# A two-layer encoder trunk on one core: the depthwise taps divided anew, the first blocks in halves, the last columns apart

## The chip, the cores and the metric

The kernel runs on one core of a Trainium2 chip. Its time is the device time of one execution in microseconds (us); lower is better. In the profile PE is TensorE's matmuls (PEld its weight loads), DVE is VectorE, ACT is ScalarE, POOL is GpSimd and SP is SyncE, which here only issues DMAs.

## The reference, cut to what matters

All data are float32: 256 tokens of width 1024, two layers. Layer 0 mixes tokens by a convolution module, layer 1 by latent attention; each layer then has a PEER expert mixer, and each of the four sub-layers ends in a layer norm.

```python
def conv_module(x, w_in, b_in, w_dw, b_dw, ln_g, ln_b, w_out, b_out):
    h = x @ w_in + b_in                                    # (256, 2048)
    a, gate = jnp.split(h, 2, axis=-1)
    h = a * jax.nn.sigmoid(gate)
    h = lax.conv_general_dilated(                          # causal, depthwise, 31 taps
        h, w_dw[:, None, :], window_strides=(1,), padding=[(CONV_WIDTH - 1, 0)],
        dimension_numbers=('NWC', 'WIO', 'NWC'), feature_group_count=D_MODEL) + b_dw
    h = jax.nn.silu(layer_norm(h, ln_g, ln_b))
    return h @ w_out + b_out

for i in range(DEPTH):                                     # DEPTH = 2
    mix = conv_module(x, ...) if i % 2 == 0 else mla_mixer(x, ...)
    x = layer_norm(DEEPNORM_ALPHA * x + mix, ln1_g[i], ln1_b[i])
    ff = peer(x, peer_w_q[i], peer_sub_keys[i], peer_u[i], peer_v[i])
    x = layer_norm(DEEPNORM_ALPHA * x + ff, ln2_g[i], ln2_b[i])
```

`peer` scores 8 heads against 128 x 128 product keys, takes the best 16 experts of each head, and combines their rows of `u` and `v`; the kernel does this densely over all 16384 experts, and that is where most of its time goes.

## The kernel before, in words

**One program for each engine.** The order of each engine's work is written out by hand, in one function per engine; semaphores join them. Every engine takes its instructions strictly in that order, so an instruction that waits holds everything behind it in its program.

**The stream of weight blocks.** All weights come in 128 x 1024 blocks of 512 KB, numbered through the whole program: `conv_in` is 0 to 15, `conv_out` 16 to 23, `wq0` 24 to 39, then `u0`, `v0`, and layer 1's. SP loads block c into the landing buffer `raw[c % 3]`. ACT rounds it to a "high" half (`make_high(c)`, line 978), DVE or POOL subtracts that to a "low" half (`make_low(c)`, line 483; 503, 1667, 1671 and 1674 for the halves of the first two blocks), and PE uses both: each product is high x high, high x low and low x high. SP issues the load of block c only when block c - 3 has been read by both:

```python
sp.wait_ge(high_made, c - RING + 1)          # RING = 3
sp.wait_ge(low_made[c % RING], c // RING)
load(name, c)
```

So a low half made later is a load issued later. The finished halves lie in a ring of three or, for some blocks, in spare room ("far homes", the tile `far_homes`).

**The start.** The input x comes in four parts (`xT_in`), block 0 in two halves, block 1 in two halves. PE warms up on `ones` (line 716), projects block 0, with four more such matmuls in the middle of it, then blocks 1 to 15 (line 594). An even block holds a chunk of values, the odd one behind it the chunk's gates: eight chunks of 128 channels. ACT takes the sigmoid (line 1067), DVE multiplies (`glu`, line 1681).

**The taps.** Each chunk then needs 31 taps, one multiply-add over 256 tokens for each tap. Chunks 0 to 4 are on DVE (lines 1689 and 1691), in two lanes that alternate; the lanes share chunk 4, and line 1731 adds its two sums. Chunks 5 and 6 are on PE, as products with diagonal matrices (line 739) that ACT's queue loads (`big<-diag`, line 1055). Chunk 7 is on POOL: ACT makes each tap's product (line 1091) into one of six buffers, and POOL adds them in two alternating sums (line 512; 515 joins them). The DMAs that ACT issues behind the projection (diagonals, x, the norm's rows: lines 1055, 1073, 996) stand ahead of those products in its program.

**Between taps and norm.** PE transposes the eight chunks to rows (line 725), DVE measures them in four groups of two chunks (line 1736), normalises (line 1754); PE transposes back (line 732), ACT applies silu (line 1104) and rounds (line 1110), DVE makes the low halves (line 1763). ACT makes the highs of blocks 20 to 24 between its silu groups, POOL the lows of 17 to 21 and 23.

**conv_out and the first layer norm.** `combine_tail` (line 662) makes the tokens in two halves: half 0 of all eight blocks, then the left 512 columns of half 1, then its right 512. DVE's `layer_norm` runs add, measure, variance, centre (line 1366), reciprocal, scale (line 1370), and PE transposes x to columns (`turn_part`, line 699). ACT rounds these (line 1010), DVE makes their lows (line 1409). PE goes on with the first four blocks of `wq0` (`lead`, line 640), half 0 and then half 1. ACT's part of this stage, with `ready` = block 30 for the first norm, is

```python
std(n, 0)
if n == 0:
    highs_to(FIRST["wq0"] + LEAD["wq0"] - 1)      # to block 27
split_xT(n, 0)
if n % 2 == 0:
    highs_to(ready - 1)                           # 28, 29
    std(n, 1)
    highs_to(ready)                               # 30
...
split_xT(n, 1)
```

`std(n, 1)` gives the square root that half 1's scaling waits for, and `split_xT(n, 1)` rounds half 1's columns.

**The end.** The last norm runs the same way. DVE adds and measures half 1's right 512 columns when PE is done, then centres and scales both sides; each side is stored by a DMA of its own (lines 471 and 475).

## Time and profile before

| | us |
|---|---|
| median of three runs | 1806.12 (1806.07 to 1806.15) |
| the profiled execution's own time | 1807.27 |
| its span in the trace | 1805.5 |
| PE busy in the span | 1791.5 (99%) |
| PE weight loads | 1570.1 (87%) |
| DVE, ACT, POOL busy | 1366.3, 945.6, 212.6 |
| mean granted TensorE clock | 0.999 of full |

The span is the traced part of the profiled execution; 1.8 us of that execution lie around it. Times of single instructions below are from the span's start. PE's busy time also counts the matmuls on `ones` that fill waits, so a stage in which PE reads busy may still be one in which another engine sets the pace.

### The profile page before, as it was taken

The numbers are of one execution on the slowest core, as the hardware profiler recorded it, in microseconds if no ns is written. First come the engines' busy times: TensorE is split into PE (matmuls) and PEld (weight loads), VectorE is DVE, ScalarE is ACT, GpSimd is POOL, SyncE is SP. The second block draws the span as 40 slices with busy tenths as digits, with TensorE's granted clock in tenths as the row PEclk, the third lists the DMA queues.
The fourth block names the chain that finished last, engine by engine and source line by source line (L and its number), as shares of the span: only waits on it lengthen the run. The fifth ranks groups of instructions, "written<-read, shape, count | busy, mean of one in ns | idle before, by whom it ended". The sixth has DMA issues, their size and how long they took to land.

```text
span 1805.5 us, 28004 instructions
## 1 busy us (share of the span) xinstructions
PE 1791.5 (99%) x10622; PEld 1570.1 (87%) x10622; DVE 1366.3 (76%) x2461; ACT 945.6 (52%) x1489; POOL 212.6 (12%) x122
## 2 busy tenths in 40 slices
PE   9999999999999999999999999999999999999998
PEld 9889998888888888888888899988888888888886
DVE  7975999888986665666666669998889866666665
ACT  5565445555555455555535454555555554555552
POOL 6720930000000000000004048000000000000000
PEclk9999999999999999999999999999999999999999
DMA  7544555555556566667733346555555566666772
GB/s 240 184 152 153 186 174 168 165 172 166 169 171 211 192 195 195 199 219 245 241 111 116 111 152 195 170 161 171 165 175 164 175 212 196 193 192 207 220 217 79
DMA packets 89413, 323.89 MB, mean 179 GB/s; under 512 B 10048, under 2 KB 10560, under 8 KB 89024
## 3 DMA queue, kind: packets, MB, share of 16 engines
q1 hardware_dynamic: 85248, 307.42, 53.3%
q10 hardware_dynamic: 4032, 14.68, 2.3%
q8 instruction: 85, 1.39, 0.3%
q14 instruction: 48, 0.39, 0.1%
HBM read 321.01 MB, written 1.05 MB: 178 GB/s over the span
## 4 chain that ended last, share of the span: by engine, by line
PE 89%; DVE 7%; DMA 1%; issue 1%; ACT 1%; POOL 0%; SPq 0%; DVEq 0%; ACTq 0%
PE y L662 40%; PE work L553 19%; PE work L556 10%; PE work L594 9%; PE y L934 3%; DVE y L1691 3%; PE work L612 2%; PE y L640 2%; PE work L615 1%; PE work L802 1%; PE y L907 1%; DMA raw<-conv_in 1%; DMA raw<-v 0%; DVE far_homes L483 0%; DMA raw<-u 0%
## 5 line engine op out<-in xcount | busy, mean ns | idle before, releaser
L483 DVE TENSOR_TENSOR low<-raw,high 128x1024 fp32r<-128x1024 f32 x385 | 470.6, 1224 | 136.8 <-ACT high L978 132.2
L978 ACT ACTIVATE high<-raw 128x1024 fp32r<-128x1024 f32 x431 | 453.5, 1053 | 198.3 <-PE work L556 97.6
L553 PE MATMUL work<-xT,high 128*128 128x512 f32 x1472 | 374.0, 396 | 0.1
L662 PE MATMUL y<-high,xT 128*128 128x512 f32 x1296 | 352.6, 390 | 0.0
L553 PEld LDWEIGHTS work<-xT,high 128*128 128x128 f32 x1472 | 264.1, 189 | 47.6 <-DVE low L483 0.5
L662 PE MATMUL y<-far_homes,xT 128*128 128x512 f32 x1320 | 304.8, 390 | 0.2 <-DVE xT L1603 0.2
L662 PEld LDWEIGHTS y<-far_homes,xT 128*128 128x128 f32 x1320 | 247.1, 188 | 51.7 <-DVE far_homes L483 0.6
L662 PEld LDWEIGHTS y<-high,xT 128*128 128x128 f32 x1296 | 243.0, 188 | 50.2
L1244 ACT ACTIVATE xT<-big 128x256 fp32r<-128x256 f32 x256 | 105.3, 416 | 256.8 <-PE y L662 251.4
L556 PEld LDWEIGHTS work<-xT,low 128*128 128x128 f32 x1472 | 200.8, 190 | 14.6
L556 PE MATMUL work<-xT,low 128*128 128x256 f32 x1472 | 205.0, 282 | 0.0
L662 PE MATMUL y<-low,xT 128*128 128x512 f32 x648 | 200.9, 389 | 0.0
L978 ACT ACTIVATE far_homes<-raw 128x1024 fp32r<-128x1024 f32 x149 | 156.8, 1052 | 78.9 <-DMA raw<-v 32.9
L483 DVE TENSOR_TENSOR far_homes<-raw,far_homes 128x1024 fp32r<-128x1024 f32 x118 | 144.2, 1224 | 61.8 <-ACT far_homes L978 61.6
L1603 DVE TENSOR_TENSOR xT<-big,xT 128x256 fp32r<-128x256 f32 x256 | 107.5, 424 | 97.0 <-ACT xT L1244 96.9
L594 PE MATMUL work<-xT,high 128*128 128x256 f32 x960 | 174.7, 284 | 1.7 <-POOL low L483 0.8
L594 PEld LDWEIGHTS work<-xT,high 128*128 128x128 f32 x960 | 149.8, 192 | 2.9 <-POOL low L483 1.0
L662 PEld LDWEIGHTS y<-low,xT 128*128 128x128 f32 x648 | 121.6, 188 | 25.4
L594 PE MATMUL work<-xT,low 128*128 128x256 f32 x480 | 135.9, 283 | 0.0
L1234 ACT ACTIVATE cross<-work 128x512 f32<-128x512 f32 x92 | 55.0, 598 | 151.3 <-PE work L556 151.3
L483 POOL TENSOR_TENSOR low<-raw,high 128x1024 fp32r<-128x1024 f32 x46 | 112.1, 2447 | 159.8 <-ACT high L978 159.6
L594 PEld LDWEIGHTS work<-xT,low 128*128 128x128 f32 x480 | 92.2, 192 | 0.0
(208 smaller groups left out, 1818.8 us busy)
## 6 DMA issues: line engine op xcount, KB each, us to landing
raw<-u SPq DMA_DIRECT2D x256, 512.0 KB, 3.6
raw<-v SPq DMA_DIRECT2D x256, 512.0 KB, 4.3
raw<-wq SPq DMA_DIRECT2D x32, 512.0 KB, 3.7
raw<-conv_in SPq DMA_DIRECT2D x14, 512.0 KB, 4.4
aux<-ln_par ACTq DMA_DIRECT2D x9, 512.0 KB, 6.5
raw<-conv_out SPq DMA_DIRECT2D x8, 512.0 KB, 4.0
raw<-mla_out SPq DMA_DIRECT2D x8, 512.0 KB, 4.7
big<-diag ACTq DMA_DIRECT2D x6, 512.0 KB, 6.2
```

The costliest lines, as they stand in the source:

```text
L483: ops.tensor_tensor(low_at(c), raw[:, slot, :], high_at(c).bitcast(F32), ALU.subtract).then_inc(low_made[slot], 1)
L553: nc.tensor.matmul(both, w_high[:, cols], xT[:, k], start=(k == 0), stop=False)
L556: mm = nc.tensor.matmul(both[:, 0, :], w_low[:, cols], xT_high[:, k, :], start=False, stop=(k == KD - 1))
L594: mm = nc.tensor.matmul(out_, w[:, cols], m[:, k, :], start=(k == 0 and n == 0), stop=(k == KD - 1 and n == 2))
L612: nc.tensor.matmul(both, w_high[:, cols], xT[:, k], start=(k == 0), stop=False)
L662: mm = nc.tensor.matmul(y[:, 2 * h + m, :], a[:, a_slot, rows], v[:, m * 512:(m + 1) * 512], start=(start and n == 0), stop=(stop and n == 2))
L934: mm = nc.tensor.matmul(y[:, 2 * q + t // 4, cols], onehots[:, q, 2, token], onehots[:, q, part, token], start=(part == 0), stop=(part == 1))
L978: A(high_at(c), raw[:, slot, :], ACT.Copy).then_inc(high_made, 1)
L1234: A(cross[:], work[:, pair_banks(pair), T:2 * T], ACT.Copy).then_inc(cross_ok, 1)
L1244: A(xT_high[:, (c - v0) % KD, :], big[:, c - v0, :], ACT.Copy).then_inc(a_high, 1)
L1603: V.tensor_tensor(xT_low[:, n % KD, :], big[:, n, :], xT_high[:, n % KD, :].bitcast(F32), ALU.subtract).then_inc(a_low, 1)
L1691: return V.scalar_tensor_tensor(dst, padded[:, k, w:w + T], tap(k, w), total, ALU.mult, ALU.add)
```

## The change

It has four parts.

**The first blocks.** Blocks 0, 1 and 2 all come in halves, in the order x part 0, block 0 left, x part 1, block 1 left, x part 2, block 0 right, x part 3, block 1 right, then block 2's halves. PE runs left halves of blocks 0 and 1, then their right halves; the four matmuls in between are gone. ACT loads its sigmoid table ahead of the first sigmoid. The low of block 3 moves from POOL to DVE, behind DVE's first tap.

**The taps.** POOL gets chunk 6 and eleven other taps: nine of chunk 4 and the last two of chunk 7. PE gets the first 29 taps of chunk 7. DVE keeps 22 of chunk 4's 31. ACT makes the first nine products (chunk 4's) between the last blocks of the projection. A new instruction on DVE, `add_last`, joins chunk 7's two parts and its bias. The highs of blocks 17, 18 and 19 move between products.

**The first layer norm.** Half 1's left columns are added and measured ahead of `split_xT(0, 0)`; the low of block 26 (`wq0` + 2) moves from before that split to behind it, the low of block 27 from before half 1's norm to behind its first scaling.

**The end.** The last norm's half 1 is cut at column 768 instead of 512; its right 256 columns are summed in a bank of `work`.

```diff
-PE_CHUNKS = (5, 6)
-POOL_CHUNK = 7
+PE_CHUNKS = (5, 7)
+POOL_CHUNK = 6
-SHARED, SHARED_TAPS = 4, 22
+SHARED, SHARED_TAPS, SHARED_END = 4, 17, 22
+LAST_END = 29
+POOL_TAPS = ([(SHARED, _w) for _w in range(SHARED_END, TAPS)] + [(POOL_CHUNK, _w) for _w in range(TAPS)]
+             + [(PE_CHUNKS[1], _w) for _w in range(LAST_END, TAPS)])
+PRODUCTS_AT = {13: 6, 14: 8, 15: 9}
+HIGHS_AT = (12, 18, 24)
+LAST_FROM = 768
...                                        (SP)
+            def load_side(c, part, ready):
+                sp.dma_start(raw[:, c, sides[part]], blocks["conv_in"][c][:, sides[part]]).then_inc(ready, 16)
             for part in range(X_PARTS):
                 ks = slice(X_PART * part, X_PART * (part + 1))
                 sp.dma_start(xT_in[:, ks, :], x_cols[:, ks, :]).then_inc(xT_in_ok[part], 16)
+                c, side = part % 2, part // 2
+                load_side(c, side, landed[c] if side else (first_landed, second_landed)[c])
...                                        (POOL)
-            low_stage(3, FIRST["conv_out"] + 1)
+            low_stage(4, FIRST["conv_out"] + 1)
+            tap_sums(0, FOR_SHARED, 2, 0)
+            nc.gpsimd.tensor_tensor(pool_sums[:, 2, :], pool_sums[:, 2, :], pool_sums[:, 3, :],
+                                    ALU.add).then_inc(pool_step, 1)
+            tap_sums(FOR_SHARED, TAPS, 0, FOR_SHARED - 1)
+            nc.gpsimd.tensor_tensor(pool_sums[:, 3, :], products[:, last % PRODUCTS, :],
+                                    products[:, (last + 1) % PRODUCTS, :], ALU.add).then_inc(pool_last, 1)
...                                        (PE, the last half)
+                for n in range(TAIL):
+                    columns(n, 0, 512, y[:, 2, :], False, n == TAIL - 1)
+                    mm = columns(n, 512, LAST_FROM, y[:, 3, 0:LAST_FROM - 512], False, n == TAIL - 1)
+                mm.then_inc(y_left, 1)
+                for n in range(TAIL):
+                    columns(n, LAST_FROM, D, work[:, 0, 0:D - LAST_FROM], n == 0,
+                            n == TAIL - 1).then_inc(block_used, 1)
...                                        (PE, the taps)
-                for w in range(TAPS):
+                end = (TAPS, LAST_END)[c]
+                for w in range(end):
...
-            pe.wait_ge(pe_conv_ok, 2)
+            pe.wait_ge(conv_done, SHARED + 2)
             to_rows(PE_CHUNKS[1]).then_inc(rows_mm, 1)
...                                        (ACT)
-                make_high(t + RING)
+                if 0 < t < 2 * KD - 2:
+                    highs_to(t + RING)
+                if t in PRODUCTS_AT:
+                    products_to(PRODUCTS_AT[t])
...                                        (DVE)
+            def add_last():
+                k = PE_CHUNKS[1]
+                dve.wait_ge(pe_conv, 2)
+                dve.wait_ge(pool_last, 1)
+                V.scalar_tensor_tensor(conv[:, k, :], y[:, 1, 0:T], conv_p[:, C_BDW + k:C_BDW + k + 1],
+                                       pool_sums[:, 3, :], ALU.add, ALU.add).then_inc(conv_done, 1)
             for g in range(GROUPS):
+                if g == 2:
+                    add_last()
...
                     scale(sides[0])
+                    if n == 0:
+                        low_stage(FIRST["wq0"] + 3, FIRST["wq0"] + LEAD["wq0"])
                     centre(sides[1])
...
                 layer_norm(n, 0, end, bias_in=(layer == 0))
+                layer_norm(n, 1, end, bias_in=(layer == 0), left=True)
+                split_xT(n, 0)
                 if layer == 0:
                     low_stage(FIRST["wq0"] + 2, FIRST["wq0"] + 3)
-                if layer == 1:
-                    layer_norm(n, 1, end, left=True)
-                split_xT(n, 0)
-                if layer == 0:
-                    low_stage(FIRST["wq0"] + 3, FIRST["wq0"] + LEAD["wq0"])
-                    layer_norm(n, 1, end, bias_in=True, left=True)
                 layer_norm(n, 1, end, bias_in=(layer == 0))
```

DVE's program around the first layer norm, from the scaling of half 0 to the splits of half 1. Before (line 483 is a low half: here of blocks 26 and 27; 1358 adds, 1363 measures, 1366 centres, 1370 scales, 1409 splits):

```order
L1370 SCALAR_TENSOR_TENSOR x<-x,stats,aux 128x1024 [waits vector_step]
L483 TENSOR_TENSOR far_homes<-raw,far_homes 128x1024 [waits high_made]
L1409 TENSOR_TENSOR xT<-work,xT 128x4x128 [waits xT_high_made] x2
L483 TENSOR_TENSOR far_homes<-raw,far_homes 128x1024 [waits high_made]
L1358 TENSOR_TENSOR x<-x,y 128x512 [waits second_half_left_columns_combined]
L1363 BN_STATS stats<-x 128x6 [waits vector_step]
L1358 TENSOR_TENSOR x<-x,y 128x512 [waits block_used]
L1363 BN_STATS stats<-x 128x6 [waits vector_step]
L1388 BN_AGGR stats<-stats 128x2 [waits vector_step]
```

Now (489 is a low half, 1420 adds, 1426 measures, 1429 centres, 1433 scales, 1464 is the reciprocal, 1479 splits):

```order
L1420 TENSOR_TENSOR x<-x,y 128x512 [waits second_half_left_columns_combined]
L1426 BN_STATS stats<-x 128x6 [waits vector_step]
L1479 TENSOR_TENSOR xT<-work,xT 128x4x128 [waits xT_high_made] x2
L489 TENSOR_TENSOR far_homes<-raw,far_homes 128x1024 [waits high_made]
L1420 TENSOR_TENSOR x<-x,y 128x512 [waits block_used]
L1426 BN_STATS stats<-x 128x6 [waits vector_step]
L1455 BN_AGGR stats<-stats 128x2 [waits vector_step]
L1457 TENSOR_SCALAR stats<-stats 128x1 [waits vector_step]
L1429 SCALAR_TENSOR_TENSOR x<-x,stats,aux 128x512
L1464 RECIPROCAL stats<-stats 128x1 [waits std_made,vector_step]
L1433 SCALAR_TENSOR_TENSOR x<-x,stats,aux 128x512 [waits vector_step]
L489 TENSOR_TENSOR far_homes<-raw,far_homes 128x1024 [waits high_made]
```

The low of block 26 has gone from ahead of the splits to behind them, and the low of block 27 from ahead of half 1's sums to behind the scaling that waits for ACT's square root. ACT's rows for this stage read the same before and now.

ACT's program from the last gate of the projection to the products behind it. Before (1067 is the sigmoid, 978 a high, 1055, 1073 and 996 DMAs, 1091 a tap's product):

```order
L1067 ACTIVATE big<-work,big 128x256 [waits block_used]
L978 ACTIVATE high<-raw 128x1024 [waits block_used,block_landed_0]
L1055 DMA big<-diag 128x896
L1055 DMA big<-diag 128x1024 x3
L1073 DMA x<-x_rows 128x1024 x2
L996 DMA aux<-ln_par 128x1024 x3
L1091 ACTIVATE big<-big 128x256 [waits glu_made]
L1091 ACTIVATE big<-big 128x256 x5
L1091 ACTIVATE big<-big 128x256 [waits pool_step] x2
L978 ACTIVATE far_homes<-raw 128x1024 [waits block_landed_1]
```

Now, from the first product on (1127 is the sigmoid, 1020 a high, 1095, 1136 and 1038 DMAs, 1116 a product):

```order
L1116 ACTIVATE big<-big 128x256 x5
L1116 ACTIVATE big<-big 128x256 [waits pool_step,block_used]
L1116 ACTIVATE big<-big 128x256 [waits pool_step]
L1127 ACTIVATE big<-work,big 128x256 [waits block_used]
L1116 ACTIVATE big<-big 128x256 [waits pool_step]
L1095 DMA big<-diag 128x896
L1095 DMA big<-diag 128x1024 x3
L1136 DMA x<-x_rows 128x1024 x2
L1038 DMA aux<-ln_par 128x1024 x3
L1116 ACTIVATE big<-big 128x256 [waits pool_step,glu_made]
L1116 ACTIVATE big<-big 128x256 [waits pool_step] x2
L1020 ACTIVATE high<-raw 128x1024 [waits block_used,block_landed_2]
```

Chunk 4's nine products stand ahead of the nine DMAs, chunk 6's products behind them, as chunk 7's did; the first moved high stands behind chunk 6's third product.

## Rows read from the trace of the kernel before

**Rows 1.** Waits of PE over the span: waiter, releaser: us, times, longest.

```profile
PE work L725 <- DVE big L1731: 1.6, 1, 1.6
PE work L699 <- DVE x L1370: 0.6, 1, 0.6
```

**Rows 2.** Chain that ended last, 0 to 110 us: start, duration, work.

```profile
17.63 0.50 DVE big L1681
...
85.57 0.42 DVE big L1731
```

**Rows 3.** Timeline of all engines, 14 to 19 us: start, busy, operation, count [idle before].

```profile
14.68 1.06 ACT L978 ACTIVATE high<-raw 128x1024 fp32r<-128x1024 f32 x1 [1.69 <-DMA raw<-conv_in]
...
18.25 0.51 PE L594 MATMUL work<-xT,high 128*128 128x256 f32 x2 [0.81 <-POOL low L483]
```

**Rows 4.** Timeline of DVE, 16 to 110 us.

```profile
68.91 7.92 DVE L1691 SCALAR_TENSOR_TENSOR y<-big,y 128x256 f32<-128x256 f32 x20
...
85.90 2.08 DVE L1736 BATCH_NORM_STATS2 big<-work 128x6 f32<-128x256 f32 x6
```

**Rows 5.** Timeline of PE at the taps' end.

```profile
79.99 4.48 PE L739 MATMUL y<-big 128*128 128x256 f32 x20
```

**Rows 6.** Timeline of ACT at the projection's end.

```profile
56.72 0.33 ACTq L1055 DMA_DIRECT2D big<-diag  x1
...
59.93 1.96 ACTq L996 DMA_DIRECT2D aux<-ln_par  x3
62.51 3.43 ACT L1091 ACTIVATE big<-big 128x256 f32<-128x256 f32 x8 [4.46 <-DVE big L1681]
```

**Rows 7.** Timeline of POOL, 14 to 100 us.

```profile
63.99 19.93 POOL L512 TENSOR_TENSOR big<-big 128x256 f32<-128x256 f32 x29 [9.32 <-ACT big L1091]
84.67 4.66 POOL L483 TENSOR_TENSOR low<-raw,high 128x1024 fp32r<-128x1024 f32 x2
```

**Rows 8.** Tile raw, 80 to 125 us: the eleven loads of 512 KB.

```profile
DMA to landing us min/median/max: 3.4/3.8/4.5
```

**Rows 9.** Timeline of ACT, high of block 20; then around the first norm.

```profile
92.26 1.05 ACT L978 ACTIVATE far_homes<-raw 128x1024 fp32r<-128x1024 f32 x1
...
118.07 1.06 ACT L978 ACTIVATE high<-raw 128x1024 fp32r<-128x1024 f32 x1 [1.61 <-DMA raw<-wq]
120.59 0.20 ACT L1004 ACTIVATE stats<-stats 128x1 f32<-128x1 f32 x1 [1.45 <-DVE stats L1389]
121.85 1.06 ACT L978 ACTIVATE high<-raw 128x1024 fp32r<-128x1024 f32 x1 [1.06 <-DMA raw<-wq]
122.94 0.60 ACT L1010 ACTIVATE xT<-work 128x512 fp32r<-128x512 f32 x1
```

**Rows 10.** Timeline of DVE around the first norm.

```profile
111.97 1.28 DVE L1370 SCALAR_TENSOR_TENSOR x<-x,stats,aux 128x1024 f32<-128x1024 f32 x1
...
116.26 1.22 DVE L483 TENSOR_TENSOR far_homes<-raw,far_homes 128x1024 fp32r<-128x1024 f32 x1
117.40 0.68 DVE L1358 TENSOR_TENSOR x<-x,y 128x512 f32<-128x512 f32 x1
```

**Rows 11.** Timeline of PE: `wq0`'s leading blocks, half 1.

```profile
124.48 5.73 PE L640 MATMUL y<-far_homes,xT 128*128 128x512 f32 x24
```

**Rows 12.** Timeline of DVE and SP at the end.

```profile
1798.08 0.69 DVE L1359 SCALAR_TENSOR_TENSOR x<-x,y 128x512 f32<-128x512 f32 x1 [3.80 <-PE y L662]
...
1802.27 0.75 DVE L1370 SCALAR_TENSOR_TENSOR x<-x,stats,aux 128x512 f32<-128x512 f32 x1
```

**Rows 13.** DMA issues, 80 to 125 us: KB each, median us to landing.

```profile
big<-keys ACTq DMA_DIRECT2D x1, 128.0 KB, 2.0
```

**Rows 14.** Timeline of PE: matmuls on ones at the start and behind the taps.

```profile
1.45 4.63 PE L716 MATMUL y<-ones 128*128 128x128 f32 x20 [1.45 <-POOL ones L496]
...
86.75 3.74 PE L716 MATMUL y<-ones 128*128 128x128 f32 x32
```

**Rows 15.** Windows at the end: us, length, busy of each engine, granted clock, DMA.

```profile
1802.00:1803.00 1.00, 0.00 (x0) 0.00 (x0) 0.96 (x2) 0.00 (x0) 0.00 (x0) 0.74 0.55 211
```

More of the change, by code:

```diff
@@ L689, in combine_tail, with columns @@
                 mm.then_inc(y_half, 1)
-                combine_second_half(part, norm, range(TAIL), TURN_AFTER[min(norm, 1)], wait_half)
+                if norm < 2 * DEPTH - 1:
+                    combine_second_half(part, norm, range(TAIL), TURN_AFTER[min(norm, 1)], wait_half)
+                    return
+                def columns(n, lo, hi, out_, start, stop):
+                    w_high, w_low = high_at(first + n), low_at(first + n)
+                    for i, (a, v) in enumerate(((xT_high, w_high), (xT_high, w_low), (xT_low, w_high))):
+                        mm = nc.tensor.matmul(out_, a[:, n, P:2 * P], v[:, lo:hi],
+                                              start=(start and i == 0), stop=(stop and i == 2))
+                    return mm
+                for n in range(TAIL):
[5 more added lines that the diff above has]
+                            n == TAIL - 1).then_inc(block_used, 1)
             def turn_part(n, h, part):
@@ L719, in _ @@
             keep_clock(WARM_START)
-            project("conv_in", splits=1)
+            for side in range(2):
+                for c in range(2):
+                    for k in range(PART * side, PART * (side + 1)):
+                        if c == 0 and k % X_PART == 0:
+                            wait_xT(1 + k // X_PART)
+                        if k == 0:
+                            pe.wait_ge(left_low, c + 1)
+                        elif k == PART:
+                            wait_low(c)
+                        cols = slice(k * P, (k + 1) * P)
+                        for n, (w, m) in enumerate(((high, xT_high), (high, xT_low), (low, xT_high))):
+                            mm = nc.tensor.matmul(work[:, c, 0:T], w[:, c, cols], m[:, k, :],
+                                                  start=(k == 0 and n == 0), stop=(k == KD - 1 and n == 2))
+                    if side == 1:
+                        mm.then_inc(block_used, 1)
+            project("conv_in", 2)
             pe.wait_ge(consts, 4)
@@ L1380, in layer_norm @@
                     dve.wait_ge(y_left, n + 1)
-                    step(add(sides[0]))
-                    measure(0)
+                    step(add(whole if len(pieces) == 3 else sides[0]))
+                    for m in range(len(pieces) - 1):
+                        measure(m)
                     return
@@ L1659, in _, with low_side @@
             left = slice(0, D // 2)
+            right = slice(D // 2, D)
+            def low_side(c, side):
+                cols = (left, right)[side]
+                if side == 0:
+                    dve.wait_ge(left_high, c + 1)
+                else:
+                    dve.wait_ge(high_made, c + 1)
+                V.tensor_tensor(low[:, c, cols], raw[:, c, cols], high[:, c, cols].bitcast(F32),
+                                ALU.subtract).then_inc((left_low, low_made[c])[side], 1)
             for part in range(X_PARTS):
@@ L1717, in next_tap @@
                 else:
-                    step_before(tap_sum(k, w, total, start, conv[:, k, :] if w == TAPS - 1 else total))
+                    step_before(tap_sum(k, w, total, start, out_))
             glu(0)
-            for _ in range(AHEAD):
+            for n in range(AHEAD):
                 next_tap(0)
                 dve.wait_ge(v_step, count[0])
+                if n == 0:
+                    make_low(dve, V, RING)
             glu(1)
```

191 lines of the change are left out of this document (99 added, 92 removed).

## The prediction

> **What bounds the kernel now.** I read the page first: PE is busy 99% of the span, so a gain must be a wait of PE that goes, a filler that goes, or work of PE that goes. The view of PE's waits comes second and is short [rows 1]: 1.6 us for the taps to end, 0.6 us in the first layer norm. But PE reads busy while it fills time, so the chain of waits comes third. It runs through DVE's taps from 17.63 us until 85.57 us [rows 2]: in that stretch DVE sets the pace, and PE's next real work, `conv_out`, starts when the norm behind the taps is done. From there the chain is PE's to the end of the span, but for the first layer norm and the last microseconds. A shift of the conv stage therefore goes through to the end, unless something later swallows it. The last view is the timelines of the five engines around each place that the change touches.
>
> **The start.** PE's wait for block 3's low ended at 18.25 us; the block had landed by 14.68 us [rows 3]. A low costs POOL 4.66/2 = 2.33 us and DVE about 1.2 us [rows 7, 10]. With the load of block 3 issued some 0.5 us later, but fewer loads ahead of it in flight, I let it land as before: high 14.7 to 15.7, low on DVE to 17.0. PE gains 1.2 us. DVE's first product and tap ended at about 18.7 us (17.63 + 0.50 + 0.60); its second tap now starts at 17.0, behind the low: it gains 1.8 us. Bounds: 0.5 us if the load lands 1.3 us later, 2.7 us if earlier.
>
> **The taps.** DVE has nine fewer taps, at 7.92/20 = 0.40 us [rows 4]: 3.5 us. With the start its taps end at about 80.6 instead of 85.57 us. PE's last taps ended at 79.99 + 4.48 = 84.47 us [rows 5]; two fewer are 0.9 us, its earlier start 1.2, a small wait for `glu` 0.2: 82.1 us. So far the stage is 4 us shorter. POOL is what I expect last. ACT's nine DMA issues ran from 56.72 to 61.89 us and its products only then, the first sum 1.5 us behind [rows 6, 7]. The nine shared products pass ahead of those DMAs, chunk 6's thirty-one do not. PE's last projection block now ends near 55.2 us, the issues at 60.5, the first of the 29 sums starts at 62.0. The high behind the third product (1.06 us, less what the ring of products covers) costs 0.6 us. 29 sums at 0.69 us are 19.9: 82.5 us; the sum for chunk 7 makes it 83.2, and the joining of chunk 6 makes it 83.9. Before it ended at 84.67 [rows 7]. Now PE's rows of chunks 6 and 7 and `add_last` stand behind POOL: transposes to 84.6, two measurements at 0.35 us [rows 4], 85.4. Before, DVE's measurements ended at 88.65 us (eight of them behind 85.90, the last two for 0.75 in all). Stage: 3.3 us shorter; bounds 2.3 (POOL ends as before) and 4.2 (POOL in time). `add_last` (0.5 us) hides under POOL.
>
> **What eats part of it.** POOL's lows of blocks 17 to 19 start at 83.9, only 0.8 us earlier, and the load of block 20 waits for the first. That low ends at 86.2; with 3.8 us to land [rows 8] the block is there at 90.0. ACT, 3.3 us early, wants it at 92.26 - 3.3 = 89.0 [rows 9], between two silu groups. So ACT's program is 2.4 us early from there, and 2.0 us behind block 21 by the same sum. PE has time in hand at the second silu group, but little at the low of block 23, which stands behind ACT and POOL: PE ends half 0 some 2.3 us early, and DVE, whose own work there follows ACT's silu, starts the first layer norm 2.0 us early. Take 2.0, bounds 0.8 and 3.3. DVE ends half 0's scaling at 111.25 instead of 113.25 [rows 10].
>
> **The first layer norm: this is the step that decides.** The edit saves DVE's 1.3 us of left-side sums from the end of the path, and PE's wait of 0.6 us [rows 1] with them. It does so by making two lows later, and each low frees a landing buffer. Block 29's load waits for the low of 26, block 30's for the low of 27; ACT's program has the high of 29 ahead of half 1's square root, and the high of 30 ahead of half 1's rounding. The trace shows both highs already waiting for their loads, 1.6 and 1.1 us, with little to spare behind them: the second ends just before the rounding at 122.94 [rows 9]. Step by step from 111.25: left add and measurement 1.3, splits 1.3, low of 26 1.15: 115.0. SP issues; 3.9 us: 118.9. High 1.06 and square root 0.2: 120.2. Reciprocal and scaling 0.95: 121.15. Low of 27, now right behind: 122.3. SP issues, 3.9 us: 126.2. High 1.06: 127.3. ACT rounds the left columns 0.64, DVE splits them 0.7: 128.6 us. At that time PE can start `wq0`'s leading blocks for half 1, which it started at 124.48 us [rows 11]. It is done with half 0's, and the transposes behind them, by about 124.0 (its last block waits for the low of 27), and has nothing else in its program. So PE loses 4.1 us against today, where it came in 2.3 early. A second sum agrees: the low of 27 ended at 117.4, it now ends at 122.3, 4.9 later; the wait for PE's transposes hid about 0.5. Bounds: with loads of 3.4 us and 3.3 us from the conv stage, 2.0; with loads of 4.5 us and 0.8, 6.7. The other layer's norm has its sums in this order already and its lows elsewhere, so nothing moves there.
>
> Behind that point PE has hardly a wait in the whole trace and no filler that could be given up, so the 4.1 us stay.
>
> **The end.** PE's last 24 products of 512 columns become 48 of 256; at 0.12 instead of 0.23 us each that is 0.3 us more. DVE's add behind PE falls from 512 to 256 columns, 0.69 us [rows 12] to about 0.42, and the measurement by as much: 0.55 less. Centring and scaling touch 1024 columns twice either way: no change. DVE ended at 1803.02 (1802.27 + 0.75), the span at 1805.5: 2.5 us for a store of 256 KB. 128 KB took 2.0 and 512 KB 3.8 us [rows 8, 13], so the store of 384 KB should take 3.1 us from about 1801.8, behind the scaling of 768 columns, and ends at 1804.9, the small one behind it. Together 0.5 us saved; bounds 0 and 1.0.
>
> **Sum.** + 4.1 - 0.5 = + 3.6 us on the profiled execution's own time, 1807.27: 1810.9. The median of the runs is 1.15 below that execution, so 1806.12 + 3.6 = 1809.7 us.
>
> **The clock.** The granted clock was at its upper level, 2.4 GHz, while PE worked, and it fell after PE had ended at 1798.06: the window from 1802 to 1803 shows 0.74 [rows 15], about half of it at either level, so the fall came near 1802.5, 4.4 us behind PE's last work. PE's new wait is of that kind: idle 1.7 and 0.7 us in half 0, then from 124.0 to 128.6. What a lower clock costs is seen at the start: twenty records of `ones` took 4.63 us, thirty-two later ones 3.74 [rows 14], 0.23 against 0.12 each, so 2.3 us were lost on the twenty; 2.5 is my price. The Trainium skill, TensorE: Matmul & The Clock Gate, section HAM oscillation, says that waits for DMA between bursts of matmuls throttle the array again, so that each burst starts cold; by it this wait would be paid twice. The trace agrees where PE stops at the end, and no row of before shows so long a wait in the middle.
>
> **The rivals.**
> 1. The clock falls in the new wait. For it: [rows 15], a fall behind a pause of 4.4 us, where this one is 4.6; against: loads that land a few tenths sooner would end the pause before such a fall. Price 2.5 us: 1812.2.
> 2. The gain of the conv stage is larger: POOL's sums are fed in time, because ACT's DMA issues do not hold up its products. Then PE and DVE set 84.4 us, POOL's lows and the loads behind them come 4 us early, and the stall shrinks to 1.9: 1807.5. Against it: [rows 6], where no product stands among the issues. It decides if chunk 6's first product starts before 57 us.
> 3. The two loads are not waited for, because their landing is covered. Then the norm yields what its order promises: 2.3 + 0.5 us early at half 1, 0.5 at the end: 1802.8, faster by 3.3 us, and with rival 2 past 1802. It needs both loads to land within about 1 us of the lows; against it stand 3.4 us at least [rows 8].
> 4. The conv stage gains almost nothing, since POOL ends later than before (each high between products delays it): 1811.
>
> **How the numbers follow.** What a measurement of this kernel can tell from no change is 0.2%, 3.6 us: the limits are 1802.5 and 1809.7. My forecast, the stall without the clock, has 0.50, and lies on the upper limit, so I give half of it to each side. Rival 1 has 0.22, rival 2 0.11, rival 3 0.09, rival 4 0.08. Slower: 0.25 + 0.21 + 0.07 = 0.53; faster: most of rival 3, 0.08; the rest, 0.39, is no change that can be told. The range goes from 1806.3 (rival 2 with short loads) to 1812.9 (rival 1 with long loads); my own case alone is 1808.2 to 1811.5.
>
> **What the profile of the changed kernel would show.** DVE's taps end near 80.6 us, PE's near 82, POOL's last join near 84; if POOL ends before 82, the sum of the taps is wrong. ACT's high of block 20 waits for its landing by about 1 us. Around the first norm, ACT's highs of 29 and 30 wait 3 us and more for DMA, PE's wait before half 1's leading blocks is 4 to 5 us, and its start is near 128.6 us. If that start is before 125 us I am wrong altogether. The granted clock behind it reads 1.00 or below: that is rival 1. At the end DVE's last scaling stands 4.3 us behind PE's last product instead of 5.0.

## The result and the profile after

The changed kernel took 1826.82 us (median of 4 runs, 1825.99 to 1828.24) beside 1806.13 us for the kernel before on the same chip: ratio 1.0112, 95% interval 1.0098 to 1.0126. It is 20.7 us slower. The prediction was 1809.7 us with a range up to 1812.9: the sign was right, the size was far outside. The profiled execution has a span of 1823.9 us (before 1805.5).

The waits of PE over the span (waiter, releaser: us in total, times, longest) are the place to begin; these four of them answer to [rows 1]:

```profile
PE work L766 <- DVE big L1812: 12.9, 1, 12.9
PE y L649 <- DVE xT L1479: 3.7, 1, 3.7
PE work L725 <- DVE x L1433: 1.7, 1, 1.7
PE y L649 <- DVE far_homes L489: 0.5, 1, 0.5
```

The second line is the wait that the prediction called the deciding one. The first was not foreseen at all: PE waits 12.9 us for DVE's last addition behind the taps (L1812). The timeline of DVE in that stretch (start, busy, operation, count) shows what DVE was at; it answers to [rows 4] and [rows 2]:

```profile
75.80 14.71 DVE L1763 SCALAR_TENSOR_TENSOR y<-big 128x256 f32<-128x256 f32 x1
90.43 2.83 DVE L1763 SCALAR_TENSOR_TENSOR y<-big,y 128x256 f32<-128x256 f32 x7
94.14 0.42 DVE L1812 TENSOR_TENSOR big<-big,y 128x256 f32<-128x256 f32 x1
97.06 0.76 DVE L1817 BATCH_NORM_STATS2 big<-y 128x6 f32<-128x256 f32 x2
```

One tap took 14.71 us. The view of line 1763 alone (durations in ns, minimum/median/maximum, then first and last start) shows how odd that is among its kind:

```profile
L1763 DVE SCALAR_TENSOR_TENSOR y<-big,y x135: 476/483/491, 16.8 to 93.6; 128x256 f32<-128x256 f32 x135
L1763 DVE SCALAR_TENSOR_TENSOR y<-big x1: 14715/14715/14715, 75.8 to 75.8; 128x256 f32<-128x256 f32 x1
```

Its inputs differ: 135 taps read the padded chunk in `big` (SBUF) and the running sum in `y` (PSUM). This one reads the padded chunk and GpSimd's nine summed taps of chunk 4, so both of its inputs are in `big`. GpSimd's timeline answers to [rows 7]:

```profile
62.73 19.24 POOL L516 TENSOR_TENSOR big<-big 128x256 f32<-128x256 f32 x28 [0.62 <-ACT big L1116]
81.93 0.72 POOL L525 TENSOR_TENSOR big<-big 128x256 f32<-128x256 f32 x1
82.61 0.72 POOL L528 TENSOR_TENSOR big<-big 128x256 f32<-128x256 f32 x1
83.29 4.63 POOL L489 TENSOR_TENSOR low<-raw,high 128x1024 fp32r<-128x1024 f32 x2
87.89 2.34 POOL L489 TENSOR_TENSOR far_homes<-raw,far_homes 128x1024 fp32r<-128x1024 f32 x1
```

GpSimd works without a pause until 87.89 + 2.34 = 90.23 us, and the tap ends at 75.80 + 14.71 = 90.51 us, 0.28 us later. The windows (start and end, length, busy of PE, PEld, DVE, ACT, POOL, then granted clock, DMA share, GB/s) put the two side by side, and show the price that PE pays on top:

```profile
75.80:90.50 14.70, 5.95 (x33) 4.97 (x31) 14.70 (x3) 4.54 (x8) 14.42 (x15) 0.83 0.24 74
86.00:98.00 12.00, 2.77 (x12) 2.38 (x13) 11.75 (x21) 0.00 (x0) 4.22 (x2) 0.50 0.41 131
```

In the tap's time GpSimd ran 15 instructions, for 14.42 of the 14.70 us. Behind it PE's granted clock is 0.50, its lower level (1.2 GHz), after PE had been idle from 81.75 us on; the 32 matmuls on ones take longer than the 3.74 us of [rows 14], and `conv_out` starts at 103.91, where it had started at 93.64:

```profile
94.62 0.69 PE L766 MATMUL work<-ident,big 128*128 128x128 f32 x2 [12.87 <-DVE big L1812]
96.82 4.89 PE L742 MATMUL y<-ones 128*128 128x128 f32 x32
103.91 0.71 PE L671 MATMUL y<-high,xT 128*128 128x512 f32 x2
```

The second loss is in the first layer norm. All engines around it, of the same trace, beside [rows 9], [rows 10] and [rows 11]:

```profile
122.60 1.28 DVE L1433 SCALAR_TENSOR_TENSOR x<-x,stats,aux 128x1024 f32<-128x1024 f32 x1
131.96 1.06 ACT L1020 ACTIVATE high<-raw 128x1024 fp32r<-128x1024 f32 x1 [4.70 <-DMA raw<-wq]
138.76 1.06 ACT L1020 ACTIVATE high<-raw 128x1024 fp32r<-128x1024 f32 x1 [5.65 <-DMA raw<-wq]
141.17 8.47 PE L649 MATMUL y<-far_homes,xT 128*128 128x512 f32 x24 [3.72 <-DVE xT L1479]
```

ACT's two highs wait 4.70 and 5.65 us for their loads, and half 1's leading blocks start at 141.17 instead of 124.48 us: 16.7 us late, of which 10.6 were there when DVE had scaled half 0 (its scaling ends at 123.88 against 113.25) and 6.1 are the norm's own. The blocks then take 8.47 instead of 5.73 us, 2.7 more; the granted clock reads 0.50 from 141 to 147 us, most of their time.

### The profile page after: what moved, and what is told of

Same layout as the page of the kernel before. It is cut to its first block, busy times and chain, and to the rows that moved or that the text cites. A ratio compares the mean times of both kernels' runs of the same rounds, so it can differ in the third digit from the quotient of the medians.

```text
span 1823.9 us, 28054 instructions
## 1 busy us (share of the span) xinstructions
PE 1794.6 (98%) x10634; PEld 1573.9 (86%) x10634; DVE 1380.3 (76%) x2457; ACT 949.8 (52%) x1501; POOL 214.9 (12%) x129
## 4 chain that ended last, share of the span: by engine, by line
PE 91%; DVE 6%; ACT 1%; DMA 1%; issue 1%; SPq 0%; POOL 0%; DVEq 0%
PE y L671 39%; PE work L566 19%; PE work L603 11%; PE work L569 10%; DVE y L1763 4%; PE y L976 3%; PE work L621 2%; PE y L649 2%; PE work L624 1%; PE work L844 1%; PE y L949 1%; PE y L707 0%; DMA raw<-wq 0%; DMA raw<-conv_in 0%; PE y L892 0%
## 5 line engine op out<-in xcount | busy, mean ns | idle before, releaser
L566 PEld LDWEIGHTS work<-xT,high 128*128 128x128 f32 x1472 | 264.2, 189 | 47.1
L671 PE MATMUL y<-far_homes,xT 128*128 128x512 f32 x1284 | 296.5, 390 | 0.2 <-POOL far_homes L489 0.2
L671 PEld LDWEIGHTS y<-far_homes,xT 128*128 128x128 f32 x1284 | 240.6, 188 | 50.2 <-POOL far_homes L489 0.6
L569 PE MATMUL work<-xT,low 128*128 128x256 f32 x1472 | 205.1, 282 | 0.0
L603 PE MATMUL work<-xT,high 128*128 128x256 f32 x928 | 168.1, 284 | 0.2 <-DVE low L489 0.2
L603 PEld LDWEIGHTS work<-xT,high 128*128 128x128 f32 x928 | 144.8, 192 | 0.4 <-DVE low L489 0.4
L603 PE MATMUL work<-xT,low 128*128 128x256 f32 x464 | 131.5, 283 | 0.0
```

The costliest lines, as they stand in the source:

```text
L566: nc.tensor.matmul(both, w_high[:, cols], xT[:, k], start=(k == 0), stop=False)
L569: mm = nc.tensor.matmul(both[:, 0, :], w_low[:, cols], xT_high[:, k, :], start=False, stop=(k == KD - 1))
L603: mm = nc.tensor.matmul(out_, w[:, cols], m[:, k, :], start=(k == 0 and n == 0), stop=(k == KD - 1 and n == 2))
L671: mm = nc.tensor.matmul(y[:, 2 * h + m, :], a[:, a_slot, rows], v[:, m * 512:(m + 1) * 512], start=(start and n == 0), stop=(stop and n == 2))
```

## The experiments

The kernel before was run again with each group of runs; its medians were 1806.73 us beside the first four, 1806.38 beside the next four and 1806.60 beside the last three. Theory A: an instruction of DVE that takes two operands from SBUF, as the tap does, gets no turn while GpSimd's instructions follow each other without a pause. Its rival is that the tap waited for something of its own (its semaphore, or the way it is made). The first runs put the two against each other, the later ones sized the rest of the change; each expectation names its theories in its own words.

**The sum kept out of SBUF inputs** (`sum_by_psum`). The changed kernel, with the shared chunk's second sum begun by an ordinary first tap, and GpSimd's sum added at the end to a sum in PSUM:

```diff
-                if (k, w) == (SHARED, SHARED_TAPS):
-                    dve.wait_ge(pool_step, FOR_SHARED - 1)
-                    total = pool_sums[:, 2, :]
...
+            dve.wait_ge(pool_step, FOR_SHARED - 1)
+            step(V.tensor_tensor(total_of(0, 2), total_of(0, 2), pool_sums[:, 2, :], ALU.add))
```

> The changed kernel, but DVE's 18th tap of chunk 4 starts a sum of its own instead of reading GpSimd's sum; that sum is added behind the taps by one instruction that reads PSUM and SBUF. Theory A (the tap read two operands from SBUF and could not run beside GpSimd's back-to-back instructions): no DVE instruction of the taps over 0.6 us, the taps end near 80 us instead of 93.9, PE's wait of 12.9 us and the low clock behind it go, the time falls by 14 to 16 us to about 1811 to 1812. Theory B (the tap waited for GpSimd's sum itself, or for its products): the wait moves to the new addition, and the time stays near 1826.

Measured: 1817.86 us (4 runs), ratio 1.006 (1.0044 to 1.0075), 9.0 us faster than the changed kernel, not 14 to 16. DVE's timeline, then GpSimd's:

```profile
75.81 0.48 DVE L1761 TENSOR_SCALAR y<-big 128x256 f32<-128x256 f32 x1
86.20 0.39 DVE L1833 BATCH_NORM_AGGREGATE big<-big 128x2 f32<-128x24 f32 x2
86.62 4.98 DVE L1835 TENSOR_SCALAR big<-big 128x2 f32<-128x2 f32 x1
```

```profile
64.04 19.25 POOL L516 TENSOR_TENSOR big<-big 128x256 f32<-128x256 f32 x28 [0.62 <-ACT big L1116]
84.61 4.67 POOL L489 TENSOR_TENSOR low<-raw,high 128x1024 fp32r<-128x1024 f32 x2
```

The tap takes 0.48 us, but the gain is smaller than expected, because the wait moved. An instruction on 128x2 numbers from SBUF to SBUF (0.26 us before) now stands in GpSimd's three lows and ends at 91.60, where they end at 91.57 us. It is small and has one input, so neither the size nor a second input is needed.

To read SBUF alone is not enough either. The first tap at 75.81 us has its only input in SBUF (it writes PSUM) and took 0.48 us in the middle of GpSimd's 28 sums, and the two instructions at 86.20 us read and write SBUF in the middle of a low and took 0.39 us together. The kernel before shows the same at 178 us, where the search for the largest scores runs from SBUF to SBUF beside a low:

```profile
178.77 2.41 POOL L483 TENSOR_TENSOR low<-raw,high 128x1024 fp32r<-128x1024 f32 x1 [7.67 <-ACT high L978]
179.09 0.48 DVE L1428 MAX8 big<-big 128x8 f32<-128x128 f32 x2
```

So what was held are instructions with two tensors from SBUF and this TENSOR_SCALAR from SBUF to SBUF; what sets the latter apart, no run here tells.

**The old first layer norm on top of it** (`sum_by_psum_old_norm`): in layer 0 the left-side sums, `split_xT(n, 0)` and `low_stage` stand in the order of before.

> As the run before, and the first layer norm in its old order (lows of blocks 26 and 27 ahead of half 1's sums). If the two late loads cost what was forecast, this is 6 to 9 us faster than the run before (6.4 us of waits, and up to 2.7 us of the lower clock behind them), near 1803, faster than the kernel before by 2 to 3 us. If the norm's order is harmless and the wait there came from the disturbed stage ahead of it, both runs are equal.

Measured: 1811.30 us (10 runs), ratio 1.0025 (1.0016 to 1.0035). The new order of the first norm costs 6.6 us here, as expected; the time of 1803 us that I expected with it did not come, since the 4.97 us wait on 128x2 numbers is still there.

**GpSimd with pauses** (`pool_pauses`): the changed kernel, where each of GpSimd's sums waits until its predecessor has ended.

```diff
-                    if w >= 4:
-                        pool.wait_ge(pool_step, done + w - 3)
+                    if w >= 3:
+                        pool.wait_ge(pool_step, done + w - 2)
```

> The changed kernel, but each of GpSimd's tap sums waits until the one before it is complete, which puts a short pause between them; nothing on DVE is changed. Theory A1 (the tap gets its turn when GpSimd pauses between two instructions): the tap of 14.7 us takes under 1.5 us, GpSimd's sums take 1 to 4 us more in all, the time falls by 12 us or more. Theory A2 (it gets its turn only when GpSimd has nothing left in its program that is ready): it still takes over 10 us and ends when GpSimd's lows end.

Measured: 1819.94 us (1 run), 6.9 us faster than the changed kernel, not 12 or more. DVE, then GpSimd:

```profile
76.52 0.48 DVE L1763 SCALAR_TENSOR_TENSOR y<-big 128x256 f32<-128x256 f32 x1
92.68 2.22 DVE L1836 TENSOR_SCALAR big<-big 128x2 f32<-128x2 f32 x1
```

```profile
74.05 14.84 POOL L516 TENSOR_TENSOR big<-big 128x256 f32<-128x256 f32 x17 [0.50 <-POOL big L516]
90.21 4.67 POOL L489 TENSOR_TENSOR low<-raw,high 128x1024 fp32r<-128x1024 f32 x2
94.83 2.36 POOL L489 TENSOR_TENSOR far_homes<-raw,far_homes 128x1024 fp32r<-128x1024 f32 x1
```

The same instruction, with both inputs in SBUF and the same semaphore, takes 0.48 us beside a GpSimd that pauses. That bears out theory A, in the form that a pause lets DVE in, and the rival falls: nothing of the tap's own was changed. The pauses are not free: a sum then comes every 14.84/17 = 0.87 us instead of 0.69, and PE waits 7.4 us for GpSimd. The 128x2 instruction was held here too, but only until the second of the three lows ended (94.88 us; it ended at 94.90), though the third followed without a visible pause.

**The suspect put into the kernel before** (`two_sbuf_in_before`): in the kernel before, two first taps take a start value from SBUF, one before and one in GpSimd's row of sums. Their sums hold a wrong start value.

```diff
+                if start and (k, w) in ((2, 0), (SHARED, SHARED_TAPS)):
+                    return V.scalar_tensor_tensor(dst, padded[:, k, w:w + T], tap(k, w), value_gate[:, 0, :],
+                                                  ALU.mult, ALU.add)
```

> The kernel before with two single instructions of DVE changed: the first tap of chunk 2 (at 42 us, where GpSimd's lows have gaps of 0.3 us and more) and the first tap of lane 1's part of chunk 4 (at 77.7 us, where GpSimd runs without a gap until 91.6) take their start value from a tile in SBUF instead of none; so those two sums hold a wrong start value. Theory A: the first takes 0.5 to 2.7 us (to GpSimd's next gap), the second some 14 us, to GpSimd's first gap at 91.6, so that the whole kernel is slower by 10 us or more. If two operands in SBUF do not matter, both take 0.5 us and the time is that of before.

Measured: 1813.0 us (1 run), 6 us slower than before with nothing else changed. DVE, then GpSimd:

```profile
41.36 0.85 DVE L1689 SCALAR_TENSOR_TENSOR y<-big 128x256 f32<-128x256 f32 x1
77.30 6.48 DVE L1689 SCALAR_TENSOR_TENSOR y<-big 128x256 f32<-128x256 f32 x1
```

```profile
63.55 19.93 POOL L512 TENSOR_TENSOR big<-big 128x256 f32<-128x256 f32 x29 [9.32 <-ACT big L1091]
83.56 0.79 POOL L515 TENSOR_TENSOR big<-big 128x256 f32<-128x256 f32 x1
```

I had expected the wait to last through GpSimd's lows, to about 91.6 us. It ended at 83.78, because GpSimd pauses for 0.08 us at 83.48: line 515 waits for the sum before it. So DVE does not need a long rest; this gap of 0.08 us let it in. The other changed tap, at 41.36 us, ended 0.29 us behind a low of GpSimd that was followed by a gap of 0.31 us.

**GpSimd yields** (`pool_yields`): the kernel with the PSUM sum and the old norm, where GpSimd waits behind its first low until DVE has normalised the first group.

```diff
+                if c == OUT_LOWS_POOL[0]:
+                    pool.wait_ge(norm_ok, 1)
```

> The kernel with the sum added by way of PSUM and the old norm order, and GpSimd waits behind its first conv_out low until DVE has begun to normalise (a pause of GpSimd where DVE's small instructions on SBUF alone come). If those instructions wait for a pause of GpSimd, the 128x2 variance instruction of 4.97 us takes under 0.6 us, PE's wait of 4.0 us ahead of the columns' transposes goes and the clock stays up: 4.5 to 7 us faster than without the pause (1811.3), so 1804 to 1807, at or below the kernel before. If that instruction was slow by itself, the time stays at 1811 or rises with GpSimd's delay.

Measured: 1807.75 us (11 runs), ratio 1.001 (1.0001 to 1.0019), 3.6 us faster than the same kernel without the wait (3.2 if each is set against the kernel before of its own group; I had expected 4.5 to 7): a wait added to one engine made the kernel faster. DVE:

```profile
86.94 0.29 DVE L1835 TENSOR_SCALAR big<-big 128x2 f32<-128x2 f32 x1
```

Yet it is no faster than the kernel before. PE now waits for GpSimd's last sum, which is what the prediction expected to be last:

```profile
PE y L768 <- POOL big L528: 2.4, 1, 2.4
```

Behind that wait the granted clock reads 0.50 from 86 to 88 us, and the 32 matmuls on ones take 5.32 us instead of 3.74.

**The first norm's new order alone, in the kernel before** (`before_new_norm`):

> The kernel before with nothing changed but the order around the first layer norm (half 1's left sums earlier, the lows of blocks 26 and 27 later). If the two late loads are the cost, PE's waits there grow from 0.6 to 6 us or more, ACT's highs of blocks 29 and 30 wait 4 to 6 us each for their loads, and the time rises by 5 to 9 us, to 1811 to 1815. If the disturbed stage ahead made that loss in the changed kernel, the time is that of before or 0.5 us less.

Measured: 1814.55 us (4 runs), ratio 1.0043 (1.0027 to 1.0058), 8.2 us slower. PE and its wait:

```profile
130.09 7.04 PE L640 MATMUL y<-far_homes,xT 128*128 128x512 f32 x24 [3.71 <-DVE xT L1411]
```

Half 1's leading blocks start 5.6 us late and take 1.3 us longer.

**The last columns apart, alone** (`before_new_end`): the kernel before with the cut at 768.

> The kernel before with nothing changed but the last norm's cut at column 768. Forecast 0.5 us faster (bounds 0 and 1.0): DVE's last scaling ends 4.3 to 4.5 us behind PE's last product instead of 5.0, PE's products take 0.3 us more, the last store lands sooner by 0.1 to 0.3. Against it: the store of 384 KB is the last to land and takes the gain away.

Measured: 1806.24 us (11 runs), ratio 1.0 (0.9991 to 1.0009). No change that can be told, though in the trace DVE's last scaling ends 4.5 us behind PE's last product instead of 5.0, as forecast.

**The clock held up** (`ones_in_wait`): the `sum_by_psum` kernel with matmuls on ones in the first norm's two waits.

```diff
+                    if turn and norm == 0 and m == blocks[-1] - 1:
+                        keep_clock(9)
...
+                if layer == 0:
+                    keep_clock(14)
```

> The kernel with the sum added by way of PSUM, still in the new norm order, and PE works on ones while it waits around the first norm (9 such products ahead of half 1's first transposes, 14 ahead of half 1's leading blocks). Theory: the waits there let the granted clock fall to its lower level, which costs 2.5 us or so behind them. Then the granted clock stays at 1.00 from 120 to 150 us, the 24 leading products of half 1 take 5.6 us instead of 7.3, and the time falls by 2 to 4 us from 1817.9. If the low clock costs nothing the time stays.

Measured: 1818.22 us (4 runs), ratio 1.0062 (1.0047 to 1.0078), beside 1817.86 without them. The clock did stay up: it reads 1.00 from 118 to 146 us, where without the ones it reads 0.68 to 0.89 between 126 and 142 us. The blocks show it, in this kernel and, in the second fence, without the ones:

```profile
135.18 5.73 PE L649 MATMUL y<-far_homes,xT 128*128 128x512 f32 x24 [0.66 <-DVE xT L1483]
```

```profile
135.43 7.29 PE L649 MATMUL y<-far_homes,xT 128*128 128x512 f32 x24 [2.42 <-DVE xT L1479]
```

The profiled executions differ by 3.9 us in span, but the medians do not: the profiled one of `sum_by_psum` was the slowest of its four (1822.29 us). That its clock fell and that of the others did not is no way out. The mean granted clock over the four was 0.995 to 0.997, and it was 0.995 in the slowest as in the fastest (1817.76 us); with the ones it was 0.997 to 0.999. So with the ones the clock was on the whole higher, and the median did not move. The expected 2 to 4 us are missed, and what the fall costs in an average run stays open.

**DMA issues behind the products** (`rows_late`): `pool_yields`, where ACT issues the loads of x's rows and of the norm's rows behind the last product, not ahead of chunk 6's first.

```diff
-            for h in range(HALVES):
-                act.dma_start(x[:, h, :], x_rows[h]).then_inc(x_in, 16)
-            ln_rows(0)
...
                 if n == COPY_AT:
                     copy_conv()
+            for h in range(HALVES):
+                act.dma_start(x[:, h, :], x_rows[h]).then_inc(x_in, 16)
+            ln_rows(0)
```

> The kernel of the run where GpSimd yields (own sum in PSUM, old order of the first layer norm, GpSimd's lows behind the normalisation), with one edit more: the two DMAs of x's rows and the three of the layer norm's rows, 3.9 us on ScalarE's queue (57.40 to 61.36 in that run), are issued behind the last product instead of ahead of chunk 6's first one. Theory (the 0.6 to 1.3 us that the divided taps bring less than they should are GpSimd's late start, made by these five issues): first sum of chunk 6 on GpSimd at 58.7 to 59.5 instead of 62.94, GpSimd's taps end at 80.4 to 81.2 instead of 84.89, TensorE's wait of 2.4 us for them goes, TensorE's own taps (82.5) set the end, the measurements end at 84.9 instead of 87.2, and the run takes 1.5 to 3 us less: 1804.5 to 1806.2. Rival (the wait is hidden anyway: what is gained at 85 is lost at the loads or the lows of the weights before 111): the measurements come 2 us sooner and the time stays at 1807 to 1808.

Measured: 1805.53 us (11 runs) beside 1806.60, ratio 0.9994 (0.9985 to 1.0003). That is 2.2 us better than `pool_yields` (2.4 against the kernel before of each group) and the best of all variants, but not to be told from the kernel before. GpSimd's last sum and PE's behind it:

```profile
81.00 0.74 POOL L528 TENSOR_TENSOR big<-big 128x256 f32<-128x256 f32 x1
```

```profile
89.87 0.70 PE L673 MATMUL y<-high,xT 128*128 128x512 f32 x2
102.60 1.67 PE L673 MATMUL y<-far_homes,xT 128*128 128x512 f32 x6 [1.18 <-POOL far_homes L489]
122.98 5.72 PE L651 MATMUL y<-far_homes,xT 128*128 128x512 f32 x24
```

`conv_out` starts 3.8 us earlier than in the kernel before (93.64), half 1's leading blocks only 1.5 us (124.48). PE no longer waits for GpSimd's last sum, and the clock stays at 1.00 there. Of the gain at the taps more than half is given back on the way, in part to the wait for GpSimd's lows, which now come too late.

**The same edit on the changed kernel** (`after_rows_late`):

> The changed kernel with the same one edit: ScalarE issues the DMAs of x's rows and of the layer norm's rows behind the last product. If VectorE's tap with both operands in SBUF waits until GpSimd pauses, it ends with GpSimd's stretch, whenever that ends: 4.0 to 4.3 us sooner (86.2 to 86.5 instead of 90.51), and the run takes 4 to 5 us less, 1822 to 1823. If the tap had a fixed cost of its own (14.7 us from its issue), its end would stay at 90.5 and the time at 1826 to 1827.

Measured: 1825.24 us (4 runs), ratio 1.0103 (1.0088 to 1.0119), 1.6 us faster than the changed kernel (2.1 against the kernel before of each group), not 4 to 5. DVE, then GpSimd:

```profile
76.53 12.38 DVE L1763 SCALAR_TENSOR_TENSOR y<-big 128x256 f32<-128x256 f32 x1
```

```profile
86.27 2.35 POOL L489 TENSOR_TENSOR far_homes<-raw,far_homes 128x1024 fp32r<-128x1024 f32 x1
```

GpSimd ends at 88.62 us and the tap at 88.91, again 0.29 us behind. The size of my expectation was off (GpSimd's row ended 1.6 us sooner, not 4, since chunk 6's sums stand behind the shared ones, which GpSimd ended only at 60.3), but the tap's end moved with GpSimd's, which is what the run was for.

**The same edit on the kernel before** (`before_rows_late`):

> The kernel before with the same one edit. There VectorE's own taps (last add at 85.57, TensorE waits 1.6 us for it) set the end of the stage and GpSimd's sums end at 84.7, 0.9 us ahead of it, so an earlier GpSimd brings nothing there: 1805.8 to 1806.8, no change. The rival, that these issues stand in the way of something else than GpSimd's start (the loads of the diagonals, say), would give it 1 to 3 us less, as in the run beside it.

Measured: 1806.24 us (11 runs), ratio 0.9998 (0.9989 to 1.0007). No change, as expected. But the reason is a plainer one: the first of GpSimd's 29 sums starts at 64.25 us (63.99 before), so the DMA issues did not hold it there. ACT's first product waits for DVE's multiplication in both: it starts at 62.51 us, 0.04 us behind it, in [rows 6] and at 62.77 us, 0.03 us behind it, here.

## Why the prediction was wrong

**The step that failed** is in the taps: "DVE has nine fewer taps, at 7.92/20 = 0.40 us". The count was right, and so was the price for the 135 taps that read a sum in PSUM. I priced the tap that starts from GpSimd's sum by the row of its neighbours, which read PSUM, and did not ask where its second input lies. The runs showed 14.71 us in place of 0.48: 0.48 us where GpSimd pauses or the start value is not in SBUF, and an end 0.28 to 0.29 us behind the instruction of GpSimd that a pause follows otherwise. Put alone into the kernel before, the same form of tap was held for 6.48 us and the kernel was 6 us slower (one run). Of my terms that was none, and no rival held it.

The trace of before had a sign of it. Two instructions of DVE of 128x1024 with both tensors in SBUF, beside GpSimd's lows, stand in this view of line 1766 of the kernel before:

```profile
L1766 DVE SCALAR_TENSOR_TENSOR x<-x,aux x2: 2102/2215/2328, 94.8 to 97.9; 128x1024 f32<-128x1024 f32 x2
```

That is 2.2 us where the same size took 1.28 in [rows 10]. They were held for one low each, not for a row of them: GpSimd's two lows there are 93.39 to 95.79 and 95.75 to 99.14 us, the first of the two ends at 96.87, and GpSimd's second low took 3.39 us instead of 2.36, so it was held in its turn. The Trainium skill, SBUF — State Buffer, section "SBUF: two separate sides", says that VectorE and GpSimd share one pair of ports as an exclusive lock, that a VectorE operation with two SBUF inputs or in a 2-port perf mode takes part in it, and that the loser blocks fully until the other's instruction is over. The traces agree that it blocks (14.71 us), and in the two instructions above they agree on one instruction of GpSimd as well. The tap goes beyond it: by the page it would have lost one instruction of GpSimd, 0.7 us; it lost all 15 in a row. In which mode the 128x2 instruction ran, no run here shows.

**The other steps of the stage.** PE's taps ended at 81.75 us (82.1 predicted), GpSimd's sums at 83.3 (83.9). With the tap and the 128x2 wait mended, `pool_yields` has the measurements end at 86.5 us (predicted 85.4, before 88.65), with GpSimd last as forecast: 2.2 us shorter than before, where I had 3.3 and a lower bound of 2.3. The cost of the tap in the profiled changed kernel is, by my estimate, its 14.2 us, less the 3 that DVE would have had in hand before GpSimd's end, plus 1.1 us between measurements and `conv_out` at the lower clock (103.91 - 97.82 = 6.09 against 93.64 - 88.65 = 4.99): 12.3 us.

**The first layer norm** was the deciding step of my forecast and went by it almost to the digit, and not by luck: from half 0's scaling on, each step of the path came within 0.7 us of its forecast. From DVE's scaling of half 0 to half 1's leading blocks I had 128.6 - 111.25 = 17.35 us; the trace has 141.17 - 123.88 = 17.3. The waits of the two highs, "3 us and more", were 4.70 and 5.65. Alone in the kernel before the order costs 8.2 us, since there the conv stage's gain does not stand against it, and the clock falls too.

**Rival 1** (the clock falls in the new wait) came true in the profiled changed kernel on top of my case: 8.47 instead of 5.73 us is 2.7, for which I had 2.5. But it rested on a pause as long as the 4.4 us of [rows 15], and the clock fell behind shorter ones: 3.7 us here, 2.4 us in `sum_by_psum`. And the medians with and without the ones do not show the price. The rule of the Trainium skill that the prediction weighed (TensorE: Matmul & The Clock Gate, section HAM oscillation) agrees with these rows too: a granted clock of 0.50 behind each of the two long waits, of which the second goes back to a load and the first does not. Rival 2 (ACT's DMA issues do not hold up its products) is out for the changed kernel: the issues end at 59.80 us, chunk 6's first product starts at 59.91, and moving the issues is worth 2.2 us once the tap is mended. The forecast of the changed kernel held on this point, but it misread the kernel before, whose products waited for DVE's multiplication ([rows 6]), as `before_rows_late` shows. Rival 3 is out: both loads were waited for. Rival 4 (the conv stage gains almost nothing) came near in `pool_yields`: `conv_out` starts there at 93.00 us, 0.6 us early.

**The end.** I took 0.5 us with a lower bound of 0; the scaling moved by that much in the trace, but alone the new end brings nothing that 11 runs can tell.

**The account** from medians: 1826.8, less 9.0 for the tap (the wait moved on to another instruction), less 6.6 for the norm's order, less 3.6 for that second wait, less 2.2 for the DMA issues, is 1805.4: the rest of the change (fewer taps on DVE, the start, the end) leaves the kernel about where it was. The last two steps were taken between groups of runs; set against the kernel before of each group, the steps are 9.6, 6.6, 3.2 and 2.4. They were taken in this order only, so they are no independent prices. Of my slower forecast only the 6.6 were foreseen.

**What stays open.** Between two of GpSimd's lows that follow each other without a visible pause, DVE's 128x2 instruction sometimes got in and sometimes did not. In the kernel before, `before_new_norm`, `before_rows_late` and `pool_pauses` it was issued during the second of the three lows and got in when that one ended; in `sum_by_psum`, `sum_by_psum_old_norm` and `ones_in_wait` it was issued during the first and waited for all three. No run tells what decides it. Nor was the start timed alone.

## What to carry to other kernels

Before an operand is moved from PSUM to SBUF, or GpSimd is given a long row of work, list what VectorE issues in that time and mark each instruction that takes two tensors from SBUF, and the short TENSOR_SCALAR from SBUF to SBUF. The price of such an instruction is not its own row's duration: it can be all the time to GpSimd's next pause. The remedy is cheap: keep one input in PSUM, or let GpSimd wait once at the place where VectorE's short instructions stand. A duration copied from a neighbour row holds only if the operands lie in the same memories.

## What the runs showed of the hardware

- A VectorE SCALAR_TENSOR_TENSOR with both tensors in SBUF was held for a whole row of GpSimd's instructions: 14.71, 12.38 and 6.48 us on 128x256. A TENSOR_SCALAR on 128x2 from SBUF to SBUF was held for 4.98 us. Elsewhere the same two forms were held for one GpSimd instruction only (2.10 us on 128x1024 in the kernel before, 2.22 us on 128x2 in `pool_pauses`).
- Taps with a PSUM input ran at 0.48 us throughout. So did a TENSOR_SCALAR from SBUF to PSUM (0.48 us), two BATCH_NORM_AGGREGATE (0.39 us) and MAX8 (two in 0.48 us) from SBUF to SBUF, all beside a busy GpSimd: to read SBUF alone does not hold an instruction up.
- The held taps ended 0.28 to 0.29 us behind the GpSimd instruction that a pause followed, the 128x2 instruction 0.03 us behind it; a gap of 0.08 us was enough to let a tap in.
- A GpSimd sum of 128x256 that waits for its predecessor comes every 0.87 us, one that does not every 0.69 us.
